# Second half of the conditioning in two quarters, its weight tiles taken where they land, and some loads put in another order

## The reference, cut to what matters

```
cond = silu(c)
ada = cond @ w_ada[l] + b_ada[l]          # (2048) @ (2048, 6144)
shift, scale, gate = split(ada, 3)
h = x * (1 + scale) + shift
proj = h @ w_in[l]                        # (512, 2048) @ (2048, 6144)
... four branches: gated short convolution, dilated attention with a relative bias,
... RG-LRU after a width-4 convolution, S5 state space with GLU
y = concat(branches) @ w_out[l]
x = layer_norm(alpha * x + (1 + gate) * y)
```

## Time and profile before

| | |
|---|---|
| Median of three runs | 1693.5 us (1692.15 to 1694.27) |
| The profiled execution | 1694.41 us |
| Its span in the profile | 1692.6 us |
| TensorE busy | 1636.2 us, 97% of the span |
| VectorE busy | 1172.4 us, 69% |
| ScalarE busy | 759.2 us, 45% |
| Granted clock of TensorE, mean | 0.989 of full speed |
| HBM read | 263.89 MB |

### The profile page before, as it was taken

The page is one execution under the profiler, slowest core; times in us unless marked ns, Lnnn a source line. Parts: engine busy times, 40 slices in busy tenths (PEclk is TensorE's granted clock), DMA queues, the critical chain, the costliest instruction groups (busy, mean ns, idle before and its releaser), DMA issues.

```text
span 1692.6 us, 22915 instructions
## 1 busy us (share of the span) xinstructions
PE 1636.2 (97%) x7708; PEld 1266.6 (75%) x7708; DVE 1172.4 (69%) x2335; ACT 759.2 (45%) x994; POOL 177.5 (10%) x242
## 2 busy tenths in 40 slices
PE   5799999999999999999999999999999999999996
PEld 0347777778777777788887777777877777778885
DVE  1438976985796598668867884687388468753758
ACT  1336535554654455521127554654555465442212
POOL 2001111111111111000000111111111111100000
PEclk9899999999999999999999999999999999999998
DMA  9999899999999998878748888888988888776524
GB/s 364 358 310 229 215 225 267 221 206 239 242 226 233 246 221 199 212 275 269 236 144 212 204 199 193 207 202 205 220 204 198 190 208 201 189 185 242 180 99 113
DMA packets 316866, 372.01 MB, mean 220 GB/s; under 512 B 30536, under 2 KB 227488, under 8 KB 314080
## 3 DMA queue, kind: packets, MB, share of 16 engines
q1 hardware_dynamic: 288608, 270.57, 49.8%
q0 software_dynamic: 27504, 100.15, 33.4%
q10 hardware_dynamic: 656, 0.17, 0.0%
HBM read 263.89 MB, written 10.99 MB: 162 GB/s over the span
## 4 chain that ended last, share of the span: by engine, by line
PE 81%; DVE 9%; DMA 6%; issue 2%; ACT 1%; SPq 0%; DVEq 0%; ACTq 0%
PE bank L1332 19%; PE bank L1285 17%; PE bank L1295 17%; PE bank L1286 17%; DMA pro<-in_w_ada 3%; DVE work L1671 3%; DMA w_lo<-raw 1%; PE bank L1196 1%; DVE y_t L1679 1%; PE bank L1222 1%; PE bank L974 1%; PE bank L1210 1%; DVE ada_acc L1679 1%; PE bank L1161 1%; PE bank L1170 1%
## 5 line engine op out<-in xcount | busy, mean ns | idle before, releaser
L1285 PE MATMUL bank<-op,w_hi 128*128 128x512 f32 x1456 | 579.3, 398 | 0.0
L1286 PE MATMUL bank<-op,w_hi 128*128 128x512 f32 x1456 | 568.1, 390 | 0.0
L702 ACT ACTIVATE w_hi<-raw 128x1024 fp32r<-128x1024 f32 x187 | 198.2, 1060 | 430.5 <-PE bank L1286 256.7
L1295 PE MATMUL bank<-op,w_lo 128*128 128x512 f32 x1456 | 360.2, 389 | 0.6 <-DMA w_lo<-raw 0.5
L1285 PEld LDWEIGHTS bank<-op,w_hi 128*128 128x128 f32 x1456 | 273.4, 188 | 76.6 <-issue 18.8
L1295 PEld LDWEIGHTS bank<-op,w_lo 128*128 128x128 f32 x1456 | 272.9, 188 | 58.8 <-DMA w_lo<-raw 2.1
L1286 PEld LDWEIGHTS bank<-op,w_hi 128*128 128x128 f32 x1456 | 273.5, 188 | 56.8 <-issue 1.9
L631 POOL DMA_DIRECT2D w_lo<-raw x187 | 163.4, 874 | 1312.7 <-ACT w_lo L707 1105.7
L1332 PE MATMUL bank<-w_hi,op 128*128 128x512 f32 x960 | 232.6, 393 | 2.1 <-ACT op L906 2.1
L707 ACT ACTIVATE w_lo<-raw 128x1024 fp32r<-128x1024 f32 x185 | 195.2, 1055 | 85.9 <-PE bank L1295 84.8
L1679 DVE SCALAR_TENSOR_TENSOR ada_acc<-ada_in,cond,ada_acc 128x512 f32<-128x512 f32 x225 | 169.1, 751 | 74.5 <-DMA ada_in<-in_w_ada 55.3
(11 more groups left out here) (258 smaller groups left out, 1496.6 us busy)
## 6 DMA issues: line engine op xcount, KB each, us to landing
raw<-in_w_in SPq DMA_DIRECT2D x192, 512.0 KB, 4.8
w_lo<-raw POOLq DMA_DIRECT2D x187, 512.0 KB, 5.4
ada_in<-in_w_ada SPq DMA_DIRECT2D x256, 256.0 KB, 4.8
pro<-in_w_ada SPq DMA_DIRECT2D x32, 1024.0 KB, 9.6
raw<-in_w_out SPq DMA_DIRECT2D x64, 512.0 KB, 4.4
y_t<-in_x SPq DMA_DIRECT2D x2, 2048.0 KB, 12.8
bias_t<-bias_rows_scratch SPq DMA_DIRECT2D x16, 256.0 KB, 6.0
y_t<-in_x SPq DMA_DIRECT2D x4, 1024.0 KB, 8.1
```

Source lines behind the costliest of these rows:

```text
L702: act.activation(w_hi[:, n % NHL, :], raw[:, n % NRAW, :], ACT.Copy).then_inc(s.hi_done.sem, 1)
L1285: pe.matmul(o, w_hi[:, n % NHL, w], op_hi[k], start=k == 0, stop=False)
L1286: mm = pe.matmul(o, w_hi[:, n % NHL, w], op_lo[k], start=False, stop=False)
L1295: mm = pe.matmul(o, w_lo[:, n % NHL, w], op_hi[k], start=False, stop=k == KT - 1)
```

## The change

The second half of the conditioning (channels 1024 to 2047) is made in two quarters. Tiles 16 to 23 now hold columns 1024 to 1535 for two row blocks each, tiles 24 to 31 columns 1536 to 2047. Each is loaded by two transfers of 512 KB with rows of 2 KB, where a tile was one transfer with rows of 4 KB. Of tiles 24 to 31 those of ring slots 0 and 3 go to other memory (`pro_last`: `late`, `bias_t`, two blocks of `work`). A tile of w_in for passes 4 to 7 covers a pair of units and one quarter (4 + 4 blocks), loaded by two transfers. Passes 4 and 5 are the third quarter of both pairs, 6 and 7 the fourth; pass 6 is `newest_pair`, which takes blocks as they are modulated. Tiles, transposes and turnings of sums get new places, x's second half comes in two transfers, tiles 5 and 6 of w_in come before w_ada tiles 29 and 31, the first four ada pieces and tile 8 before the LRU and bias loads, and the bias loads wait for all w_ada tiles. S5's two sines (`angles`) move ahead of the last modulation, the S5 drives behind pass 7, `lru_gates` behind pass 8. The w_lo of pass 7 is made by VectorE.

```diff
-DVE_LO = EARLY + 3
-TURNED_AT = {(2, 4): 8, (2, 6): 9, (3, 0): 10, (3, 2): 11, (3, 3): 12, (3, 4): 13, (3, 5): 14, (3, 6): 15}
-PRO_AT = [[(1, 3, 6), (1, 3, 5, 7), (1, 3, 5, 7), (1, 2, 4, 5, 7)], [()] * EARLY]
-EARLY_TURN = ((3, 7, 4), (3, 7, 4))
+DVE_LO = EARLY_N
+KQ = KT // 4
+PAIRS = ((0, 1), (2, 3))
+PRO_ENDS = (KT, KT + 8, KT + 16)
+TURNED_AT = {(2, 2): 8, (2, 4): 9, (2, 5): 10, (2, 7): 11, (4, 1): 12, (4, 3): 13, (4, 5): 14, (4, 7): 15}
+PRO_AT = ((0, 1, 3, 6), (2, 5), (0, 3, 7), (0, 3, 7), (2, 6), (0, 3))
+SUMS_AT = {(2, 6): 1, (5, 6): 2}
+EARLY_TURN = ((3, 7, 4), (3, 7))
-FIRST_ADA_AT = (0, 0, 8, 9, 10, 11, 12, 13, 15, 16, 21, 21, 23, 23, 24, 24)
+FIRST_ADA_AT = (0, 0, 9, 9, 10, 11, 12, 13, 15, 16, 21, 21, 23, 23, 24, 24)
...
-            RAW_AT = {9: 0, 15: 1, 18: 2, 22: 3, 27: 4}
+            RAW_AT = {9: 0, 15: 1, 18: 2, 22: 3, 26: 4, 29: 5, 31: 6}
...
-                if a == 22:
-                    x_load(1)
+                if a in (22, 28):
+                    x_load(KH + KQ * (a // 28), KH + KQ * (a // 28 + 1))
...
+                else:
+                    quarter, k = a // 8, 2 * (a % 8)
+                    w = slice(quarter * D // 4, (quarter + 1) * D // 4)
+                    for i in range(2):
+                        sp.dma_start(pro_half(a, i).rearrange("p (i n) -> p i n", i=2),
+                                     w_ada_v[0, k + i, :, 0:2 * D].rearrange("p (i n) -> p i n", i=2)[:, :, w])\
+                            .then_inc(pro_in[a % PRO_RING].sem, 16)
...
-                    raw_load(0, 0, DVE_LO - 2)
+                    raw_load(0, 0, EARLY_N - 1)
                     sp.wait_ge(bias_row.sem, 1)
                     sp.dma_start(bias_rows_d, brow[:, 0, :].unsqueeze(1).to_broadcast([HEADS, REPLICAS, 640]))\
                         .then_inc(bias_io.sem, 16)
-                    lru_loads(0)
-                    sp.wait_ge(bias_io.sem, 16)
-                    bias_loads(0)
                     for place, at_half in enumerate(FIRST_ADA_AT):
                         if at_half == 0:
                             ada_loads(0, place)
+                    raw_load(0, 0, EARLY_N)
+                    lru_loads(0)
+                    sp.wait_ge(bias_io.sem, 16)
+                    sp.wait_ge(pro_used.sem, PRO_TILES)
+                    bias_loads(0)
...
+                def early_pair(n, tiles=()):
+
+                    pe.wait_ge(s.hi_done.sem, s.hi_done.at(n + 1))
+                    pe.wait_ge(s.op_hi.sem, KQ * (pair_of(n)[1] + 1))
+                    pe.wait_ge(s.op_lo.sem, KQ * (pair_of(n)[1] + 1))
+                    for j, (o, w, k) in enumerate(pair_blocks(n)):
+                        pe.matmul(o, w_hi[:, n % NHL, w], op_hi[k], start=False, stop=False)
+                        mm = pe.matmul(o, w_hi[:, n % NHL, w], op_lo[k], start=False, stop=False)
+                        if j == 2 * KQ - 1:
+                            mm.then_inc(s.hi_used.sem, 1)
+                        beside(n, j, tiles)
+                    pe.wait_ge(first_lo_done.sem, n + 1)
...
-                    put(EARLY if first else 3, s5_turn)
-                    put(EARLY + 3 if first else 6, lru_gates)
-                    for q, at in enumerate((EARLY + 2 if first else 5, EARLY + 2 if first else 5, 12, 12)):
+                    put(EARLY_N - 2 if first else 3, s5_turn)
+                    put(EARLY_N if first else 6, lru_gates)
+                    for q, at in enumerate((EARLY_N - 1 if first else 5, EARLY_N - 1 if first else 5, 12, 12)):
...
                 if first:
                     second_half()
+                    dve.wait_ge(bias_io.sem, 16)
...
-                    first_lo(EARLY)
-                    conditioning(1)
-                    for k in range(KH, KT):
+                    first_lo(EARLY + 2)
+                    conditioning(2)
+                    for k in range(KH + KQ, KT):
                         modulated(k)
-                        if k == KH + 2:
-                            first_lo(EARLY + 1)
                     all_modulated()
-                    first_lo(EARLY + 2)
+                    first_lo(EARLY + 3)
...
                     for k in range(KH):
                         modulated(k)
-                    for n in range(NHL, NHL + 2):
+                    for n in range(NHL, EARLY):
+                        first_lo(n)
+                    conditioning(1)
+                    for k in range(KH, KH + KQ):
+                        modulated(k)
+                    for n in range(EARLY, EARLY + 2):
                         first_lo(n)
```

261 lines of the change are left out of this document (155 added, 106 removed).

## The result

The changed kernel takes 1696.91 us (median of 20 runs, 1694.39 to 1701.41), the kernel before beside it 1694.66 (20 runs, 1692.15 to 1696.77): the ratio is 1.0016, 95% interval [1.0010, 1.0022]. That is 0.16% slower; by the medians it is 2.3 us or 0.13%. The profiled execution took 1695.35 us, its span is 1693.5.

A forecast was written before the change was run, and what follows sets the result against it. TensorE was taken as the bound, locked with VectorE by 177 us. Its gain of 5.8 (stop, slow clock) + 2.3 (holes) = 8.1, minus 4.8 at the lock and 1.9 for the clock, left 1.4: 1693.5 to 1692.1 us, range 1689.2 to 1695.5.

The forecast's parts named there:

- VectorE's lead: Opening up to the third scores: VectorE gains 3.3 us, as its 3.15 us wait for tile 7 of w_in goes.
- TensorE's passes: Opening, passes 0 to 7: summed prices per pass, tile and transpose put TensorE 8.1 us ahead at lru_gates.
- The halves: w_ada tiles 16 to 31 as two 512 KB transfers: 2.9 us more at 381 GB/s, inside the margin, priced at nothing.
- Rival (d): Halved w_ada tiles run slow, at 345 GB/s, and TensorE stops 3.3 us before the last tiles: 1697.8 us, chance 0.06.
- (e): Third quarter modulated over 5 us too late, so pass 4 stops: no gain, 1693.5 us, chance 0.05.
- SP's queue and piece 4: SP's loads ahead of s5_in(0): ada piece 4 lands at 135.0, wanted at 135.2, so no cost.
- rival (c): SP blocked by LRU transfers, piece 4 lands at 138.4, VectorE loses 3.2 of its 3.3 us: 1695.5, chance 0.10.
- The lock and the clock: Ahead of the third scores TensorE stops some 5 us for VectorE (minus 4.8), then loses 1.9 to 1.2 GHz.
- the slack of 0.5: TensorE's 0.49 us wait for VectorE ahead of the fourth scores in the kernel before, within which the clock might recover.
- What survives step 0 survives to the end.: After step 0 the rest of the kernel is TensorE's, so everything behind moves by the 1.4 us left.

The follow-up runs named there:

- e1: The changed kernel again, unaltered, on another chip slot: median 1696.01 us against 1695.16 for the kernel before, ratio 1.0002.
- e11: The changed kernel, unaltered, for a further profile: profiled execution 1698.38 us, s5_outputs at 227.02 us.
- e10: The kernel before with conditioning pieces 24 to 31 of the first step loaded in one partition only: 1694.57 us, ratio 0.9993.
- e16: The kernel before with two conditioning pieces moved ahead of the first normalise: ratio 1.0000 to the unaltered kernel before.
- e4: The changed kernel with the first step's third and fourth scores one weight tile later: median 1696.55 us, ratio 1.0012 to the kernel before.
- e9: The changed kernel with conditioning pieces 24 to 31 of the first step loaded in one partition only: 1695.65 us, ratio 1.0003 to the kernel before.
- e13: The changed kernel with 34 idle transposes in TensorE's stop ahead of the first step's third scores: 1699.94 us, ratio 1.0028 to the kernel before.
- e17: The changed kernel with twelve small memsets at the start of VectorE's queue, moving layer 0's loop twelve instructions later: 1693.47 us against 1695.02 before, ratio 0.9992.
- e19: The changed kernel with e15's edits, 28 transposes at the third-scores stop, and twelve memsets at VectorE's start: 1691.32 us against 1694.61 before, ratio 0.9980.
- e7: The changed kernel with idle transposes in TensorE's opening waits and ahead of pass 0: 1698.35 us, ratio 1.0011 to the kernel before.
- e8: The kernel before with the same idle transposes in TensorE's opening as e7: ratio 1.0006 to the unaltered kernel before.
- e3: The changed kernel with VectorE's conditioning pieces 4 and 5 taken behind the first scan, later pieces one place later: 1696.10 us, ratio 1.0007 to the kernel before.
- e14: The changed kernel with the edits of e7, e13 and e9 together: median 1693.28 us, ratio 0.9994 to the kernel before.
- e6: As e3, with step 0's scores, turns, weighings, copies and s5_outputs also one tile later: 1697.99 us, ratio 1.0017 to the kernel before.
- e15: The changed kernel with the idle transposes of e7 and e13 and two conditioning pieces moved ahead of the first normalise: 1693.77 us, ratio 0.9996 to the kernel before.
- e2: The changed kernel with LRU and bias loads put back ahead of the first conditioning pieces and tile 8: 1700.8 us, ratio 1.0029 to the kernel before.

## Why the prediction was wrong

The time came out 4.8 us above the 1692.1. Of these 1.2 are the base, 1694.66 over 20 runs beside the change where three runs had given 1693.5; the rest is the gain of 1.4 that turned into a loss of 2.3. Two steps failed: VectorE's lead (3.3 us in the sum, 0.5 over all profiles that show it), and the step that puts nothing behind step 0 (there the changed kernel loses 1.2 us against the kernel before). The steps in the order of the sum:

- **TensorE's passes.** Forecast starts of passes 1 to 5 were 77.1, 85.1, 96.4, 105.6 and 115.3; they came at 76.3, 84.3, 95.5, 104.7 and 114.4. The method, a price per pass, tile and transpose read from start to start, was good to 0.9 us in total.
- **The halves.** Priced at nothing, and no tile of w_ada was waited for; they came at 372 GB/s. Rival (d) and (e) are out. By the batching rule of the Trainium skill (DMA: Bandwidth & Descriptors, section Bandwidth) they should have been late; the trace, at 372 GB/s, differs. The page's figures are for transfers issued from GpSimd, and these were issued from SP.
- **SP's queue and piece 4, "no cost, but a thin cover".** Too small: I priced what stands behind the pieces and not the pieces, which took 9.44 us. SP was 1.3 us late with piece 4, and it took 0.8 longer to land than I had it: VectorE waited 1.94 us (1.71 in e1, 1.75 in e11). Half of rival (c) came true, by another transfer than I had named.
- **VectorE's lead of 3.3.** 2.2 in the first pair of profiles (144.34 to 142.12 at the first scan). Over three profiles each it is 0.2 (143.8 and 143.6). Up to that scan e10 and e16 run the kernel before's code and e4, e9 and e13 the changed kernel's; with them it is 0.5 (144.2 over five, 143.7 over six). This step failed in its base: I took pass 0's 13.61 us from one execution, and removed the very stop that swallowed a late pass 0. In the changed kernel pass 1 begins at 78.0 on average over those six, 0.9 behind my 77.1, and the scan comes 65.7 behind it, where my sum had 63.9: the 1.8 us are about piece 4's wait. The opening's low clock then passes whole into step 0.
- **The lock and the clock.** The mechanism was right: the stop was 4.17 us where I had said 5, the clock fell, and the fourth scores came at 183.63 (183.5 forecast). That hit was partly luck: VectorE let TensorE go at 175.54, 1.1 us later than forecast, and the clock took 1.5 us where I took 2.4. Its size varies: less the slack of 0.5 it is 1.0, 1.0 and 2.4 us in three profiles, where I took 1.9. TensorE's stops of 2.2 to 4.2 us for tile 8's w_lo at 141 to 146 us weren't in the sum; in nine of the fourteen profiles with the new order the clock falls there too, which shortens the stop ahead of the third scores.
- **"What survives step 0 survives to the end."** This is the step that failed in kind: my sum put nothing behind step 0. From 250 to 584 us the changed kernel loses 0.8 us on average where the kernel before gains 0.4 on the same scale. The difference, 1.2, all lies between 400 and 584. Its cause is the place of the loop in VectorE's code: e17 and e19 shift it and the loss is gone. In the first pair of profiles 0.9 us of the lead go between 400 and 584, and another 1.1 between 584 and 932, with the low clock at 700 and 892; for that part no run has a cause.

Together, over three profiles each: s5_outputs 1.3 us later on average (224.4 and 223.1; lead 0.2, minus 1.5 between the scores), plus 1.2 between 250 and 584, makes 2.5 us, beside 2.3 and 0.9 by the two comparisons of medians. That this fits is partly luck. Three executions are few, and those of the kernel before (1694.41, 1692.45 and 1692.44) all lie below the medians of that kernel beside the runs, 1694.61 to 1696.27; by the end of the span the three and three are 3.1 us apart.

Open: what makes tile 22's w_lo land 2.7 or 5.6 us after its issue (e1 and e7, e8 with a wait of 1.9 between); when the clock falls at 700 us, which it does in some profiles of either kernel, and near 890, in four of the changed one and its variants (first, e3, e4, e14); and why single executions reach 1700 us and more. Late openings and the 6.8 us of low clock make part of it (e11, 1698.38), but no run accounts for the longest.

## What to carry to other kernels

A stop that an edit removes was also a buffer: read the spread of the stage ahead of it from several profiles before counting its length as a gain, and ask which engine stands next and what the clock does there. When the times of two versions part in a loop that the edit doesn't touch, look at the first instructions behind each jump back for time marked issue, and try the same code a few instructions later before changing anything else. A lead counts only where nothing behind it waits for transfers; compare the two traces at one marker per step down to the end.

## What the runs showed of the hardware

- The loop's jump back costs VectorE 4.2 to 5.1 us in steps 2 and 3 of layer 0 (5.4 and 5.9 once each) and 3.8 to 4.9 in layer 1, with nothing to wait for. Where the body begins in the code decides on a second stop of 1.2 to 2.1 us in layer 0: there in 12 of 12 profiles (in e6 and e15 in one step of the two) with the body 8 operations later than in the kernel before, absent in 6 of 6 of that kernel and its variants, absent in 2 of 2 with 12 more. The Trainium skill (Runtime: NRT & Kernel Launch, section Instruction fetch mechanics) says that instructions are loaded in blocks of 256, that prefetch is sequential, and that a taken branch whose target isn't at hand must load it first. The trace agrees in kind; that a target a few instructions ahead of a block's end pays for two blocks would explain the second stop, but no run here measured a block's length.
- Behind a stop of 4.16 to 4.17 us ahead of the third scores the granted clock stayed at 0.50 for 3.4 us (first profile, e2) or 6.8 us (e9, e11); behind 2.34 (e1) and 2.67 us (e7) for 3.4; behind 1.85 (e3) and 1.55 us (e17) it stayed at full. With the stop filled by transposes (e13, e14, e15, e19) it stayed at full.
- The same transfer (w_lo of tile 22, 512 KB), issued 0.8 to 1.2 us behind the first of four pieces of 256 KB, was of use to TensorE 2.7 us (e1), 4.2 us (e8) or 5.6 us (e7) later.
